# Seven block products for one of four K groups in ten gate and up pairs of a two-layer kernel

## The reference

```
hn = rms_norm_2(x, norm_ffn_pre[l])
f = (jax.nn.silu(hn @ w_gate[l]) * (hn @ w_up[l])) @ w_down[l]
x = x + rms_norm_2(f, norm_ffn_post[l])
```

## Time and profile before

| | |
|---|---|
| median of 3 runs | 2546.61 us (2546.46 to 2547.21) |
| the profiled execution: its span | 2545.0 us |
| its own time beside it | no time of that one execution is on record apart from the span; the runs' median is 1.6 us above the span |
| mean granted clock of TensorE | 0.997 |
| PE busy | 2512.1 us, 99% of the span |
| DVE busy | 1848.3 us, 73% |
| ACT busy | 1256.3 us, 49% |
| DMA | 578 MB, mean 227 GB/s |

### The profile page before, as it was taken

The page is one execution under the profiler, slowest core; times in us unless marked ns, Lnnn a source line. Parts: engine busy times, 40 slices in busy tenths (PEclk is TensorE's granted clock), DMA queues, the critical chain, the costliest instruction groups (busy, mean ns, idle before and its releaser), DMA issues.

```text
span 2545.0 us, 30060 instructions
## 1 busy us (share of the span) xinstructions
PE 2512.1 (99%) x11372; PEld 2062.4 (81%) x11372; DVE 1848.3 (73%) x2387; ACT 1256.3 (49%) x1732; POOL 3.9 (0%) x11
## 2 busy tenths in 40 slices
PE   7999999999999999999999999999999999999998
PEld 6788877788878888888888888888888888888886
DVE  8999999999877677557665667666666674456665
ACT  4445677764554444444444545554544444444443
POOL 0000000000000000000000000000000000000000
PEclk9999999999999999999999999999999999999999
DMA  9999566888946656666555554445455555555553
GB/s 381 358 348 327 214 232 217 285 302 318 363 178 221 231 207 228 238 232 223 212 217 199 190 204 169 162 178 203 182 184 196 198 201 198 197 196 187 196 199 116
DMA packets 80787, 578.23 MB, mean 227 GB/s; under 512 B 9166, under 2 KB 9462, under 8 KB 10881
## 3 DMA queue, kind: packets, MB, share of 16 engines
q1 hardware_dynamic: 79056, 567.25, 61.0%
q10 hardware_dynamic: 1074, 6.37, 0.6%
q0 software_dynamic: 512, 2.69, 0.3%
HBM read 574.15 MB, written 3.70 MB: 227 GB/s over the span
## 4 chain that ended last, share of the span: by engine, by line
PE 90%; DVE 5%; ACT 2%; issue 2%; DMA 1%; DVEq 0%; ACTq 0%; SPq 0%
PE bank L784 87%; DVE wlo L1681 2%; DVE cv L1897 1%; DVE raw L1691 1%; PE bank L723 1%; DVE cv L1672 1%; DMA raw<-in_w_in 1%; ACT whi L1107 1%; ACT PR L1107 0%; PE bank L984 0%; PE bank L1027 0%; PE bank L899 0%; PE bank L1047 0%; ACT SS L1284 0%; PE bank L749 0%
## 5 line engine op out<-in xcount | busy, mean ns | idle before, releaser
L1681 DVE TENSOR_TENSOR wlo<-raw,whi 128x1024 fp32r<-128x1024 f32 x872 | 1056.3, 1221 | 561.4 <-ACT whi L1107 558.7
L1107 ACT ACTIVATE whi<-raw 128x1024 fp32r<-128x1024 f32 x872 | 911.5, 1057 | 915.0 <-PE bank L784 741.9
L784 PE MATMUL bank<-whi,HTh 128*128 128x512 f32 x2536 | 689.7, 393 | 8.0 <-ACT HTh L1107 4.8
L784 PE MATMUL bank<-wlo,HTh 128*128 128x512 f32 x2536 | 680.3, 390 | 1.5 <-DVE wlo L1681 1.5
L784 PE MATMUL bank<-whi,HTl 128*128 128x512 f32 x2536 | 680.1, 390 | 0.0
L784 PEld LDWEIGHTS bank<-wlo,HTh 128*128 128x128 f32 x2536 | 476.2, 188 | 102.9 <-DVE wlo L1681 3.3
L784 PEld LDWEIGHTS bank<-whi,HTl 128*128 128x128 f32 x2536 | 476.6, 188 | 100.6
L784 PEld LDWEIGHTS bank<-whi,HTh 128*128 128x128 f32 x2536 | 469.6, 188 | 109.1 <-issue 9.1
L1691 DVE CUSTOM_DVE_ANT_0 raw<-raw,GT,VECS 128x2048 f32<-128x2048 f32 x95 | 222.6, 2344 | 0.5 <-DMA raw<-in_w_ada 0.2
L784 PE MATMUL bank<-whi,ACTh 128*128 128x512 f32 x704 | 189.4, 389 | 0.0
L784 PE MATMUL bank<-whi,ACTl 128*128 128x512 f32 x704 | 189.4, 389 | 0.0
(11 more groups left out here) (253 smaller groups left out, 1210.5 us busy)
## 6 DMA issues: line engine op xcount, KB each, us to landing
raw<-in_w_in SPq DMA_DIRECT2D x126, 1024.0 KB, 4.9
raw<-in_w_ada SPq DMA_DIRECT2D x95, 1024.0 KB, 6.5
raw<-in_w_gate SPq DMA_DIRECT2D x88, 1024.0 KB, 4.8
raw<-in_w_up SPq DMA_DIRECT2D x88, 1024.0 KB, 4.8
raw<-in_w_down SPq DMA_DIRECT2D x88, 1024.0 KB, 4.8
raw<-in_w_o SPq DMA_DIRECT2D x16, 1024.0 KB, 6.9
raw<-in_w_out SPq DMA_DIRECT2D x16, 1024.0 KB, 4.8
raw<-in_w_attn_out SPq DMA_DIRECT2D x8, 1024.0 KB, 5.5
```

Of the source, the lines that this page charges most:

```text
L784: i = e.matmul(bank[2 * ch.st + t][:, :], (xl if ps == 1 else xh)[:, k, tk(t)], (lo if ps == 2 else hi)[:, j * 512:j * 512 + 512], start=c ...
L1107: return e.activation(dst, src, ACT.Copy, scale=scale)
L1681: e.tensor_tensor(lo, src, r32(hi), S_).then_inc(lo_done, 1)
```

## The change

In ten of the eleven gate and up pairs of the second layer (all but the first) the K group 1 of gate and up (pieces of the two units called star) is computed by a seven-product scheme. Of the group's activations A (256 tokens x 512 K, cut into 2 x 2 blocks of 128 x 256: token half by K half) and of its weights B (512 K x 1024, cut into K half by gate or up), the eight block products become seven. A block product is one piece with one left operand and one token half: two K blocks, three passes, 6 matmuls (`form`). A pair was 16 pieces of 12 matmuls; it is now 12 such pieces and 7 of 6 matmuls.

- Order of a pair (`DUO`): g is a plain piece of gate, u one of up, a number one of the seven forms. The positions in a pair are counted from 0 to 18 below. The pair's plain units are three of gate and three of up.
- The sums of weights (forms 5, 6, 7, 4) are four subtractions of 128 x 1024 on POOL, written over one half of a star unit in the raw buffer. Each form is split by ACT and DVE as any piece is.
- The sums of activations are made once: ten subtractions and additions of 128 x 256 on DVE, one copy of 128 x 1024 on ACT, one low part on DVE (`forms_left`, `forms_high`).
- Forms 1, 5, 6 and 7 add up in the banks of the up chunk; after each, ACT copies the bank (128 x 512) to SNP (`hold`, four in a pair), and PE waits for that copy before it goes on in the same bank. At the end of each chunk DVE adds bank and SNP (four in a pair), then ACT applies Silu to SNP (`gates`) and DVE multiplies (two each).
- The two star units of a pair hold two of the four raw buffers (`pinned`); the plain units of these pairs take turns in the other two.
- Gate and up of a pair have banks 0 to 3 or 4 to 7, in turn by pair. The transposes of a pair begin 7 slots after its end, not 2 (but for the last of a part). The row of norm_ffn_post is loaded later, as it shares its place with SNP.

```diff
+STAR = 1
+DUOS = (1,)
+FORMS = {1: Form((0, 0), None, 1, 1, ("A", 0, 0)),
+         2: Form((0, 1), None, 0, 0, ("A", 0, 1)),
+         3: Form((1, 1), None, 1, 0, ("S", 3)),
+         4: Form((0, 0), ((0, 1), (0, 0)), 0, 1, ("A", 1, 1)),
+         5: Form((0, 0), ((1, 0), (0, 0)), 1, 0, ("S", 0)),
+         6: Form((0, 0), ((1, 1), (0, 0)), 1, 1, ("S", 1)),
+         7: Form((1, 0), ((1, 1), (1, 0)), 1, 1, ("S", 2))}
+DUO = ["g", 1, "g", 5, "g", 6, "g", 7, "g", 4, "g", 2, "u", 3, "u", "u", "u", "u", "u"]
+HELD = {1: "s1", 5: "m5", 6: "s2", 7: "s3"}
+AFTER = {6: "s1", 7: "s2", 3: "m5"}
...
+        star = [unit(side, STAR) for side in range(2)]
+        rest = [[(g, half) for g in range(nkg) if g != STAR for half in range(2)] for _ in range(2)]
...
     def turn_slot(n, part, c):
         last = c == FCUT[part][1] // 4 - 1
-        return M[f"ffn{n}{part}"] + 16 * c + 17, 4 if last else 2
+        end = chunk_of("up", (n, part, c)).p1
+        return end + (2 if last or n not in DUOS else 7), 4 if last else 2
...
+        def form(s):
...
+            if pc.form in AFTER:
+                w.wait_ge(*held[n](*ch.j[1:], AFTER[pc.form]))
...
+            for ps in R(3):
+                if ps == 2:
+                    w.wait_ge(lo_done, s + 1)
+                for j in R(2):
+                    i = e.matmul(o, left[ps == 1][j], (lo if ps == 2 else hi)[:, j * 512:j * 512 + 512],
...
         def split(p):
             src, hi, lo = piece_aps(p)
             arrived(w, P.pieces[p].unit)
+            if p in add_no:
+                w.wait_ge(add_done, add_no[p])
...
+        def hold(p):
...
+            w.wait_ge(pe_done, p + 1)
...
+            copy(SNP[:, i, :], bank[2 * pc.chunk.st + FORMS[pc.form].t][:, :]).then_inc(*held[n].one(part, c, name))
...
+                elif ch.kind in ("gate", "up") and ch.duo:
+                    n, part, c = ch.j
+                    i = t + 2 * (ch.kind == "up")
+                    w.wait_ge(*summed(ch, t))
+                    w.wait_ge(*held[n](part, c, ("s1", "s3", "s2", "m5")[i]))
+                    e.tensor_tensor(SNP[:, i, :], B, SNP[:, i, :], A_).then_inc(emptied["DVE"], 1)
...
+        for p in adds:
+            pc = P.pieces[p]
+            (ua, ha), (ub, hb) = pc.add
+            arrived(w, ua)
+            arrived(w, ub)
+            for q in R(p - 1, pc.chunk.p0 - 3, -1):
+                if (P.pieces[q].unit, P.pieces[q].half) == (pc.unit, pc.half):
+                    w.wait_ge(lo_done, q + 1)
+                    break
+            if add_no[p] > 1:
+                w.wait_ge(add_done, add_no[p] - 1)
+            e.tensor_tensor(raw_of(pc.unit, pc.half), raw_of(ua, ha), raw_of(ub, hb), ALU.subtract).then_inc(add_done, 1)
```

More of the change, by code:

```diff
@@ L21 @@
 Unit = namedtuple("Unit", "kind src off kt n tag value")
-Piece = namedtuple("Piece", "unit half kt n chunk ks")
+Piece = namedtuple("Piece", "unit half kt n chunk ks form add")
+Form = namedtuple("Form", "raw add side t left")
+STAR = 1
[10 more added lines that the diff above has]
+AFTER = {6: "s1", 7: "s2", 3: "m5"}
 def vec_layout():
@@ L210, in plan_ffn @@
                 continue
+            if layer in DUOS:
+                st = 2 * ((c + part) % 2)
+                chs = [p.chunk(kind, (layer, part, c), f"f{layer}", "DVE", st=st + i) for i, kind in enumerate(("gate", "up"))]
+                p.duo(chs, [("w_gate" + ext, f0 // 4 + c), ("w_up" + ext, f0 // 4 + c)], 4)
+                continue
             ch = p.chunk("gate", (layer, part, c), f"f{layer}", "ACT")
@@ L760, in piece @@
                 return
+            if pc.form:
+                form(s)
+                return
+            if ch.duo and ch.kind == "up":
+                for name in ("m5", "s3"):
+                    w.wait_ge(*held[ch.j[0]](*ch.j[1:], name))
             one_pass(s, 0, 0, 1)
@@ L1173, in evict @@
                         *sq_act[n].one(ch.j, t))
-                elif ch.kind == "gate":
+                elif ch.kind == "gate" and not ch.duo:
                     n, part, c = ch.j
@@ L1213, in evict, with gates, forms_high @@
                         emptied["ACT"], 1)
+        def hold(p):
+            pc = P.pieces[p]
+            n, part, c = pc.chunk.j
+            name = HELD[pc.form]
+            i = ("s1", "s3", "s2", "m5").index(name)
+            w.wait_ge(pe_done, p + 1)
+            before = d_items.index((part, c)) - 1
+            if before < 0:
+                w.wait_ge(*res_dve[2 * n](3, 1))
+                w.wait_ge(*rows_of(2 * n, 3, 1))
+            elif i >= 2:
+                w.wait_ge(*upm[n](*d_items[before], i - 2))
+            copy(SNP[:, i, :], bank[2 * pc.chunk.st + FORMS[pc.form].t][:, :]).then_inc(*held[n].one(part, c, name))
+        def gates(n, part, c):
+            for t in R(2):
+                w.wait_ge(*empty("gate", (n, part, c), t))
+                gate_free(n, part, c)
+                if n:
+                    w.wait_ge(*res_dve[2](f"minv{t}"))
+                e.activation(SG[:, t, :], SNP[:, t, :], ACT.Silu,
+                             scale=RR[:, 2 + t:3 + t] if n else 1.0).then_inc(*silu[n].one(part, c, t))
+            yield 1
+        def forms_high(n):
+            w.wait_ge(*s_dve[n]("j"))
+            copy(SH[:, :, :], S32[:, :, :]).then_inc(*s_act[n].one("hi"))
+            yield 1
         def gate_free(n, part, c):
@@ L1660, in scalar @@
                 evict(ends[s - 1])
+            if s and s - 1 < NP and P.pieces[s - 1].form in HELD:
+                hold(s - 1)
             lane.slot(s)
@@ L2320, in vector @@
             lane.begin(slot, turned2(name, j, ops))
+        for n in DUOS:
+            lane.begin((B0, B2)[n] + 15, forms_left(n))
         for t in R(2):
```

175 lines of the change are left out of this document (157 added, 18 removed).

## The result

The kernel became slower: 2580.56 us against 2546.53 us, a ratio of 1.0135 (95% interval 1.0122 to 1.0148). Its profiled execution has a span of 2577.9 us, 32.9 us over that of the kernel before. The forecast was 2535 us and faster, with a range to 2573: the time lies outside it, on the side of rival 1.

What follows compares the result with a forecast made beforehand. PE was taken as the bound, its matmuls running without gaps. 2546.6 - 13.6 (fewer matmuls) + 0.5 (activation sums) + 1.0 (short PE waits) = 2534.5, rounded up to 2535 us; own range 2532 to 2539, whole range 2531 to 2573.

Steps and rivals of the forecast that it cites:

- rival 1: Gate and up pairs: POOL's weight sums hold up DVE's low parts, so PE waits; slower, 2567 us; chance 0.36.
- The term on PE: Ten pairs of gate and up: 6 matmuls fewer each, 60 in all, -13.6 us; a pair takes 42.2 us.
- The four sums on POOL: Weight sums in each pair: 2.3 us each on POOL, hidden up to 4 us, so no cost.
- DVE in a pair: DVE's work beside PE in each pair: 35.6 of 42.2 us, nearer 34, so zero cost.
- the chain: Start of a pair: DVE's split of form 5, POOL's sum, ACT's split of form 6; over 2 us left.
- A2: Theory tested in the experiments, no size forecast: the chain split, sum, split in a pair is too long by itself.
- one-time activation sums: Made once on DVE, 5.4 us, with an ACT copy of 1.06: cost taken as 0.5 us, bounds 0 and 2.
- ACT and the holds: ACT's work in a pair, four bank copies of 0.59 us included: 25.0 of 42.2 us, taken at nothing.
- Loads: Weight loads at a pair's end: next first unit 4.4 us late for ACT, 2.7 us to spare, zero cost.
- rival 2: Ring of two raw buffers: late loads delay the next pair's first piece; no change, 2544 us; chance 0.15.
- Rival 3: Start of each pair: POOL's sum takes over 4 us and sets the pace; 2555 to 2565 us; chance 0.05.

Runs made afterwards that it cites:

- the sums aside: Changed kernel with the same forty POOL subtractions on a tile nobody uses, waited for by no engine, weights not summed: 2576.48 us, ratio 1.0120.

## Why the prediction was wrong

**The term on PE: right, slightly too large.** 60 matmuls fewer, as 11312 instructions show. A free pair lasts 42.35 us, not 42.2, so it is 12.1 us and not 13.6; the median of the run without sums and with early activation sums is 11.2 us under before.

**The steps from there to the changed kernel**, by medians: 2535.3 us without weight sums and with early activation sums; +4.0 with the activation sums in their place (2539.2); +37.2 with the sums running on POOL, waited for by nobody (2576.5); +4.1 with the true sums and ACT's wait for them (2580.6).

**The step that failed** is "The four sums on POOL", of which the prediction says that "a sum of up to 4 us is hidden", together with "DVE in a pair ... Zero": each engine was costed alone. The runs showed 37 us in its place. The duration was right (2.3 us taken, 2.37 to 2.42 measured alone), and the slack of the chain nearly so (A2 costs about 4 us, not nothing). What was missing is that the two engines exclude each other, which stood in the text only as rival 1 with 0.36. The Trainium skill ("SBUF — State Buffer", who interferes with whom) states that rule; the runs here agree with it in each point that they can show: two inputs in SBUF are held until the sum ends (2.72 us for 1.22), one input (transposes, 0.45 us) and one in PSUM (681 ns) are not, and a POOL instruction that only writes holds nobody (1.23 us at most).

**Rival 1 was right in its second argument, not in its first.** The first was DVE's total: up to 2.3 us lost to each sum, 43.6 us in a pair, and a turning point at 1.95 us a sum. DVE lost 1.1 us a sum on average (1953.5 against 1909.9 us busy; 1.8 with the sums aside), under that point, and from 1900 to 2110 us it was busy for 171 of 210 us. The second was that the loss strikes early in a pair, where the lead is spent. That is what the traces show: PE waiting for whi and wlo at form 6, low parts up to 3.43 us, the first gate unit of the next pair late. It gave 46.5 us for each of the eight pairs that follow another; measured are 46.2 to 48.0 in seven and 43.6 in one, 24.4 us over before in all, where it had 23.5. So the size was right as well, for these eight.

**What rival 1 lacked is the first pair.** It had -1.4 us for it, and measured are +9.3. The prediction had the one-time activation sums at "Bounds 0 and 2 us; I take 0.5". The first pair lasts 10.5 us more than a free pair of 42.35 us. Without weight sums it is 4.9 us more, and with weight sums but the activation sums early 5.1 us more. The two causes add up. In the kernel after both went into one stall: the ACT copy that needs the last activation sum has a fixed place in ACT's order, in slot 16, while DVE makes that sum in its slot 16, behind nine other sums, a low part (1.21 us) and an eviction (1.40 us), and one of the sums met POOL (2.62 us for 0.42). ACT stood for 8.67 us with splits behind it (6.47 without weight sums), PE ran dry, and the clock fell.

**ACT and the holds** at nothing: right, PE never waited for a hold. **Loads**: the first gate unit did land some 4 to 5 us after ACT wanted it (predicted 4.4), and PE's lead covered it as long as DVE was on time; rival 2 alone did not happen, since no pair of the run without sums waits for it. **Rival 3** did not either: the longest sum lasted 3.33 us.

## What to carry to other kernels

Before work is given to an idle POOL, sort DVE's instructions in the same stretch by their inputs. Here a POOL subtraction of 1024 elements a partition took 2.4 us, and a DVE instruction with two SBUF inputs that met it got nothing done until it ended. On average that took 1.1 us from DVE, about what the sum would have cost on DVE itself (1.2 us), so nothing was saved; and with the sums on DVE the kernel was 23.5 us faster. An engine's busy share does not show such a loss: what counted was where in the pair it fell. A saving on the bound engine of 6 in 192 is only as good as the lead of the engines that feed it, and where halved pieces spend that lead, the place of a job (transposes at slot 2, 7 or 9: 10 and 4 us) counts as much as its cost. For each new wait, look at what stands behind it in that engine's order, also for work done only once. And before a wait is taken away, look at which wait stands behind it: it can have hidden one that is as long.

## What the runs showed of the hardware that was not expected

The exclusion works by whole instructions and in both directions: a low part of 1.22 us lasted 2.72 us, a sum of 2.40 lasted 3.3. A DVE instruction of 0.42 us (128 x 256) that met a sum took 2.62. After a wait of 7.45 us PE worked at the 1.2 GHz level for about 6 us. After the wait of 3.1 us in the run without sums it did so too, for about 3 us (granted clock 0.58 from 1869 to 1873, 1.00 before and after). After waits of 1 to 1.5 us no such stretch follows, only the first pass of four is 0.13 us longer (1.04 from start to start, against 0.91).
